# A two-layer decoder trunk on one core: softmax statistics carried between two row orders by VectorE copies instead of folding matmuls

## The reference, cut to what matters

```python
for g, (window, dilation) in enumerate(DIL_CONFIGS):
    o, l = dilated_group_attention(q[g], k[g], v[g], window, dilation, rel_table)
    outs.append(o); lses.append(l)
alpha = jax.nn.softmax(jnp.stack(lses, axis=0), axis=0)
o = jnp.sum(alpha[..., None] * jnp.stack(outs, axis=0), axis=0)
```

## Time and profile before

| | before |
|---|---|
| median of 3 runs | 1594.29 us |
| profiled execution, its own time | 1594.29 us |
| span of the profile | 1592.4 us |
| instructions | 22054 |
| TensorE matmul busy | 1576.4 us, 99% |
| VectorE busy | 919.3 us, 58% |
| ScalarE busy | 590.9 us, 37% |
| GpSimd (POOL) busy | 286.4 us, 18% |
| granted TensorE clock | 0.998 |

### The profile page before, as it was taken

One profiled execution on the slowest core, in us unless ns is written; L12 is line 12 of the kernel. 1 busy time (PEld: TensorE's weight loads), 2 busy tenths in 40 slices (PEclk: granted clock), 3 DMA queues, 4 the chain that ended last, 5 costly groups with the idle time before them and its releaser, 6 DMA issues.

```text
span 1592.4 us, 22054 instructions
## 1 busy us (share of the span) xinstructions
PE 1576.4 (99%) x8034; PEld 1296.5 (81%) x8034; DVE 919.3 (58%) x1585; ACT 590.9 (37%) x1064; POOL 286.4 (18%) x516
## 2 busy tenths in 40 slices
PE   9999999999999999999999999999999999999998
PEld 7888888888888788888888878888878888888886
DVE  5466466457456844536355766777685363545565
ACT  5324314324324522213123446676552131222344
POOL 2072473474470200000001110000020000000111
PEclk9999999999999999999999999999999999999999
DMA  6565464465443233333333332332233333333341
GB/s 166 151 166 145 141 171 129 140 166 133 120 126 112 79 104 88 100 92 97 100 92 99 99 118 69 106 92 72 73 93 98 90 104 94 92 103 92 93 116 70
DMA packets 314909, 174.84 MB, mean 110 GB/s; under 512 B 38713, under 2 KB 302450, under 8 KB 314850
## 3 DMA queue, kind: packets, MB, share of 16 engines
q1 hardware_dynamic: 300112, 158.61, 35.5%
q0 software_dynamic: 14480, 15.42, 3.5%
q10 hardware_dynamic: 258, 0.04, 0.0%
HBM read 157.11 MB, written 10.60 MB: 105 GB/s over the span
## 4 chain that ended last, share of the span: by engine, by line
PE 89%; POOL 5%; DMA 2%; DVE 1%; ACT 1%; SPq 1%; issue 0%; POOLq 0%; ACTq 0%; DVEq 0%
PE unit_out L1702 24%; PE unit_out L1704 24%; PE unit_out L1703 24%; POOL probs L902 4%; POOL sumsq L910 1%; PE attn L1850 1%; DMA w_raw<-in_a_w_qkv_dram 1%; PE attn L2098 1%; PE turned L1778 1%; PE unit_out L1869 1%; PE unit_out L1870 1%; PE unit_out L1871 1%; PE logits L1702 1%; PE misc L1778 1%; PE misc L1702 1%; PE misc L1704 1%
## 5 line engine op out<-in xcount | busy, mean ns | idle before, releaser
L1702 PE MATMUL unit_out<-act_hi,w_hi 128*128 128x512 f32 x1849 | 725.9, 393 | 1.6 <-DVE act_lo L1251 1.1
L1704 PE MATMUL unit_out<-act_hi,w_lo 128*128 128x512 f32 x1849 | 718.6, 389 | 0.0
L1703 PE MATMUL unit_out<-act_lo,w_hi 128*128 128x512 f32 x1849 | 718.0, 388 | 0.0
L928 ACT ACTIVATE w_hi<-w_raw 128x1024 fp32r<-128x1024 f32 (+3 forms) x256 | 270.9, 1058 | 464.2 <-PE unit_out L1704 368.3
L1702 PEld LDWEIGHTS unit_out<-act_hi,w_hi 128*128 128x128 f32 x1849 | 347.1, 188 | 77.3 <-DVE w_lo L1236 3.0
L1704 PEld LDWEIGHTS unit_out<-act_hi,w_lo 128*128 128x128 f32 x1849 | 347.1, 188 | 72.6
L1703 PEld LDWEIGHTS unit_out<-act_lo,w_hi 128*128 128x128 f32 x1849 | 347.4, 188 | 69.4 <-issue 0.2
L1236 DVE TENSOR_TENSOR w_lo<-w_raw,w_hi 128x1024 fp32r<-128x1024 f32 (+3 forms) x256 | 319.5, 1248 | 102.0 <-ACT w_hi L928 102.0
L902 POOL DMA_DIRECT2D probs<-blocks x448 | 220.3, 501 | 229.7 <-DVE blocks L1350 201.0
L910 POOL TENSOR_TENSOR sumsq<-sumsq,square 128x512 f32<-128x512 f32 x41 | 57.8, 1410 | 1053.6 <-ACT square L956 1051.8
L1098 ACT ACTIVATE act_hi<-hidden 128x512 fp32r<-128x512 f32 x64 | 40.5, 633 | 243.4 <-DVE hidden L1500 243.4
(11 more groups left out here) (296 smaller groups left out, 1384.2 us busy)
## 6 DMA issues: line engine op xcount, KB each, us to landing
w_raw<-in_w_ff_dram SPq DMA_DIRECT2D x128, 512.0 KB, 4.0
w_raw<-in_a_w_qkv_dram SPq DMA_DIRECT2D x56, 512.0 KB, 4.3
probs<-blocks POOLq DMA_DIRECT2D x448, 32.0 KB, 2.5
w_raw<-in_b_w_qkv_dram SPq DMA_DIRECT2D x24, 512.0 KB, 5.0
w_raw<-in_a_w_qkv_dram SPq DMA_DIRECT2D x32, 256.0 KB, 3.1
w_raw<-in_w_ple_gate_dram SPq DMA_DIRECT2D x16, 512.0 KB, 3.9
bias_tiles_b<-bias_vectors SPq DMA_DIRECT2D x16, 256.0 KB, 4.4
bias<-bias_tiles_b SPq DMA_DIRECT2D x8, 512.0 KB, 3.8
```

The lines of the kernel that those rows point to most:

```text
L928: sc.activation(weights_of(u)[0][:, 0:width, :], w_raw[par][:, 0:width, :], ACT.Copy).then_inc(hi_done, 1)
L1702: te.matmul(bank, w_k[0], hi, start=start, stop=False)
L1703: te.matmul(bank, w_k[0], lo, start=False, stop=False)
L1704: return te.matmul(bank, w_k[1], hi, start=False, stop=stop)
```

## The change

VectorE now carries the statistics by itself, in slot 2 (`merge`) and slot 4 (`near`; in the drain 4 and 6): 16 copies each, every one from 32 partitions to 32 others, of 4 elements (minimum and sum of two heads) in the first and 2 in the second. Only the last of each 16 raises a semaphore. The folds, the spreads, their waits, `fold`, `quarter` and the POOL instructions that made them are gone, and with them VectorE's waits for TensorE's folds.

```diff
-A_SPREAD, A_MERGE, A_NEAR = 1, 2, 4
+A_MERGE, A_NEAR = 2, 4
-DRAIN_SPREAD, DRAIN_MERGE, DRAIN_NEAR = 3, 4, 6
+DRAIN_MERGE, DRAIN_NEAR = 4, 6
...
+        def rows_of(a):
+
+            return slice(a * SUB, (a + 1) * SUB)
...
-            pool.memset(quarter[:, :], 0.0).then_inc(quarter_ready, 1)
-            pool.wait_ge(quarter_ready, 1)
-            for r in range(NT):
-                pool.memset(quarter[r * SUB:(r + 1) * SUB, r:r + 1], 1.0).then_inc(quarter_ready, 1)
...
-            pool.tensor_tensor(fold[:, :], ident[:, 0:SUB], ident[:, SUB:2 * SUB], ALU.add
-                               ).then_inc(fold_ready, 1)
...
-                if has_attn and i == spread_at:
+                if has_attn and i == merge_at:
 
                     wait(ve, exp_done, (s - 1).times(A_ITEMS) + 2)
-                    ve.tensor_tensor(
-                        spread_stat[:, :, :],
-                        near_stat[:, :, :].rearrange("p a b -> p (a b)").unsqueeze(2
-                            ).to_broadcast([P, 4 * NT, NT]),
-                        quarter[:, :].unsqueeze(1).to_broadcast([P, 4 * NT, NT]),
-                        ALU.mult).then_inc(spread_stat_ready, 1)
-                if has_attn and i == merge_at:
-
-                    wait(ve, far_ps, s)
-                    ve.tensor_copy(far_stat[:, :, 0, :], far_in[:, :].rearrange(
-                        "p (a b) -> p a b", a=2)).then_inc(merge_step, 1)
+                    far, near = (x.rearrange("p a (j b) -> p a j b", b=NT) for x in
+                                 (far_stat[:, :, 0, :], near_stat[:, :, :]))
+                    for b, r in itertools.product(range(NT), range(NT)):
+                        last = ve.tensor_copy(far[rows_of(b), :, :, r], near[rows_of(r), :, :, b])
+                    last.then_inc(merge_step, 1)
                     merged(s, 1)
...
                     wait(ve, share_ready, s)
-                    ve.tensor_tensor(spread_share[:, :, :],
-                                     share[:, 0, :].unsqueeze(2).to_broadcast([P, 2 * NT, NT]),
-                                     quarter[:, :].unsqueeze(1).to_broadcast([P, 2 * NT, NT]),
-                                     ALU.mult).then_inc(spread_share_ready, 1)
                 if has_attn and i == near_at:
-                    wait(ve, near_ps, s)
-                    ve.tensor_copy(near_share[:, :], near_in(has_proj)).then_inc(near_share_ready, 1)
+                    near, far = (x.rearrange("p (j b) -> p j b", b=NT) for x in (near_share[:, :], share[:, 0, :]))
+                    for b, r in itertools.product(range(NT), range(NT)):
+                        last = ve.tensor_copy(near[rows_of(r), :, b], far[rows_of(b), :, r])
+                    last.then_inc(near_share_ready, 1)
                     wait(ve, near_share_ready, s)
...
-                if has_attn and i == merge_at:
-
-                    wait(te, spread_stat_ready, s)
-                    for b in range(NT):
-                        last = te.matmul(
-                            far_in[b * SUB:(b + 1) * SUB, :].rearrange("p (a r) -> p a r", r=NT),
-                            fold[:, :],
-                            spread_stat[:, :, :].rearrange("p (a b) r -> p a b r", b=NT)[:, :, b, :],
-                            start=True, stop=True)
-                    last.then_inc(far_ps, 1)
-                if has_attn and i == near_at:
-                    wait(te, spread_share_ready, s)
-                    for r in range(NT):
-                        last = te.matmul(
-                            near_in(has_proj)[r * SUB:(r + 1) * SUB, :].rearrange("p (j b) -> p j b", b=NT),
-                            fold[:, :],
-                            spread_share[:, :, :].rearrange("p (j r) b -> p j r b", r=NT)[:, :, r, :],
-                            start=True, stop=True)
-                    last.then_inc(near_ps, 1)
```

More of the change, by code:

```diff
@@ L313, in build @@
         inv = sb("inv", [P, 4])
-        fold = sb("fold", [P, SUB])
-        quarter = sb("quarter", [P, NT])
         spare = sb("spare", [P, 1])
@@ L326, in build @@
         merge = w_raw[0][:, KC:KC + KP, :].rearrange("p k c -> p (k c)")
-        spread_stat = merge[:, 0:64].rearrange("p (a r) -> p a r", r=NT)
-        spread_share = merge[:, 64:96].rearrange("p (a b) -> p a b", b=NT)
         near_stat = merge[:, 96:112].rearrange("p (a b) -> p a b", a=2)
@@ L356, in build @@
         misc = ps("misc", [P, T])
-        far_in = logits[:, 0:4 * NT]
         def wide_bank(n):
@@ L400, in weights_of @@
             return both[:, 0, :, :], both[:, 1, :, :]
-        def near_in(has_proj):
-            return (turned if has_proj else attn)[:, 0:2 * NT]
         def scores_at(has_proj, i):
@@ L426, in merge_slots @@
         def merge_slots(has_proj):
-            return (A_SPREAD, A_MERGE, A_NEAR) if has_proj else (DRAIN_SPREAD, DRAIN_MERGE, DRAIN_NEAR)
+            return (A_MERGE, A_NEAR) if has_proj else (DRAIN_MERGE, DRAIN_NEAR)
+        def rows_of(a):
+            return slice(a * SUB, (a + 1) * SUB)
         def turned_order(x):
@@ L561, in build @@
         const_ready = sem("const_ready")
-        quarter_ready = sem("quarter_ready")
-        fold_ready = sem("fold_ready")
         gains_t = sem("gains_t")
@@ L600, in build @@
         tiles_b_ready = sem("tiles_b_ready")
-        spread_stat_ready = sem("spread_stat_ready")
-        far_ps = sem("far_ps")
         merge_step = sem("merge_step")
@@ L605, in build @@
         shift_exp = sem("shift_exp")
-        spread_share_ready = sem("spread_share_ready")
-        near_ps = sem("near_ps")
         near_share_ready = sem("near_share_ready")
@@ L860, in _ @@
                                base=0, pattern=[[-1, P]], channel_multiplier=1).then_inc(const_ready, 1)
-            pool.memset(quarter[:, :], 0.0).then_inc(quarter_ready, 1)
-            pool.wait_ge(quarter_ready, 1)
-            for r in range(NT):
-                pool.memset(quarter[r * SUB:(r + 1) * SUB, r:r + 1], 1.0).then_inc(quarter_ready, 1)
             pool.wait_ge(const_ready, 5)
-            pool.wait_ge(quarter_ready, 1 + NT)
-            pool.tensor_tensor(fold[:, :], ident[:, 0:SUB], ident[:, SUB:2 * SUB], ALU.add
-                               ).then_inc(fold_ready, 1)
[L869 to L874, removed]
             pool.memset(table_in[PIECES:PIECES + 1, :], -MASKED).then_inc(table_ready, 1)
@@ L1028, in sub_a @@
                     next_hi(u + 1)
-                _, merge_at, _ = merge_slots(has_proj)
+                merge_at, _ = merge_slots(has_proj)
                 if has_attn and i == merge_at:
@@ L1293, in start_statistics @@
             def start_statistics():
-                ve.wait_ge(quarter_ready, 1 + NT)
                 ve.wait_ge(root_ready, 1)
@@ L1332, in sub_a @@
                 start = s.reg is None and s.const == 0 and i == 0
-                spread_at, merge_at, near_at = merge_slots(has_proj)
+                merge_at, near_at = merge_slots(has_proj)
                 for ph in soft_at(has_proj, i) if has_attn else ():
@@ L1878, in sub_a @@
                 items = (s - 1).times(A_ITEMS)
-                _, merge_at, near_at = merge_slots(has_proj)
                 for ph in scores_at(has_proj, i) if has_attn else ():
@@ L1952, in sub_a @@
                     te.wait_ge(vec_ready, 4)
-                    te.wait_ge(fold_ready, NT - 1)
                 if has_proj and i == A_TURN_V[par]:
```

## The result

The changed kernel takes 1598.12 us (median of 10 runs, 1596.05 to 1600.56), the kernel before 1594.33 (10 runs, 1594.04 to 1595.57): ratio 1.0022, 95% interval 1.0014 to 1.0031. A second chip gave 1599.43 against 1594.63 (1.0028, 1.0017 to 1.0040). The forecast was 1596.7 in a range of 1591.0 to 1600.0. Two facts ask for an explanation: the profiled execution, 1596.45, lies 2.16 above its counterpart of before, almost the forecast's 2.4; and the median lies 1.7 above the profiled execution, with a spread three times that of before.

The account below looks back on a forecast made before the run. TensorE, busy 99% of the span, or what it waits for was taken as the bound, with even steps ending by POOL's chain. Odd steps -2.39, even +2.98, drain +1.78 gave +2.4 us, 1596.7, range 1591.0 to 1600.0.

Parts of the forecast that it names:

- The copy's pitch: VectorE's added copies: one at a time, 0.17 us each, so a group of 16 takes 2.7 us.
- rival 1: VectorE's copies overlap: p = 0.08, a group 1.3 us, sum -3.5, 1590.8 us; chance of faster 0.20.
- rival 2: Each VectorE copy costs p = 0.20, a group 3.2 us, sum +4.8, 1599.1 us; chance of slower 0.32.
- Even steps: Merge copies delay POOL's chain by 1.04 us: steps 2 and 4 become 1.04 longer, step 6 0.9.
- Rival 3: POOL's chain: landings spread by 1.5 us, so even steps could lose or win 1 us each by chance; no chance given.
- Odd steps: Steps 1, 5 and 7 gain 0.76 us each from two removed folds, step 3 only 0.11; sum -2.39.
- the near fold's 0.38: TensorE at the near fold: removing one fold gains 0.38 us, priced like a merge fold.
- rival 4: TensorE: the gap before a fold is not the fold's, so removal brings 0.06 us, not 0.38; chance under 0.05.
- The merge fold's 0.38: TensorE at the merge fold between two units: removing one fold gains 0.38 us.
- Near copies cost nothing: VectorE, behind the split and before the scales: later slots absorb the copies, cost nothing if p stays under 0.3.
- Drain: Last step: TensorE waits 2.22 us for scales and 0.2 for the weight split, folds give 0.64; sum +1.78.
- no difference: Outcome for the whole kernel's time, the forecast with p from 0.10 to 0.18; chance 0.48.

Follow-up runs that it names:

- e3: Changed kernel with each copy reading and writing its own 32 partitions, exchange between row orders left out: 1592.43 us, -2.30 against the kernel before.
- e11: The changed kernel unaltered, run again on another chip: 1599.43 us, +4.80 against the kernel before.
- e7: Kernel before with its folds, only the first block transposition moved to the end of slot 2: 1592.72 us, -1.75 against the kernel before.
- e8: Changed kernel with all its copies, only the first block transposition moved to the end of slot 2: 1594.98 us, +0.51 against the kernel before.
- e2: Kernel before with only the near shares carried by copies, the merge still by folds: 1597.11 us, +2.38 against the kernel before.
- e9: e6 with the near shares of steps 1 to 7 by folds again: 1589.36 us, -5.27 against the kernel before.
- e6: e5 with the first block transposition also moved to the end of slot 2: 1590.79 us, -3.68 against the kernel before.
- e5: Changed kernel with merge copies one slot earlier, before its evacuation, and the drain's near copies at slot 5's end: 1591.51 us, -2.96 against the kernel before.
- e1: Kernel before with only the merge carried by copies, the near shares still by folds: 1596.6 us, +1.87 against the kernel before.
- e10: Kernel before with 32 needless small VectorE copies added in slot 7 of each step: 1599.3 us, +4.67 against the kernel before.

## Why the prediction was right, and where it was not

**The copy's pitch** (p = 0.17, a group 2.7): measured 0.175 and 2.80. Right, and for the reason given; rival 1 (overlap) and rival 2 (p = 0.20) fell, and `e3` shows that the change of partitions decides. One detail: the first copy of a group starts on the same partitions as the instruction in front of it, so the rule of the Trainium skill holds 30 of the 32 copies of a step and not all, and the first does start 0.08 before the evacuation in front has ended (139.56 against 139.64 in step 2). It changes nothing in the sum.

**Even steps** (+1.04 by POOL's late start): the start moved by 1.07, as worked out. The step's length did not follow it everywhere, since the landing of the last block changed too: in step 2 the last issue began at 178.62 and its values at 181.99 before, 3.37 later; after, the last issue began about 0.5 before POOL's end at 179.76, and the values 1.75 later. That is -1.6, with +1.07 and 64 issues that took 0.23 less it gives the -0.78. Step 4 had like landings in both, and +0.85; step 6 became 0.39 longer and not 0.9, as POOL's issues took 0.2 and the landing 0.3 less. Rival 3 named this (1 us a step, by chance), and it took 1.6 in one. But by chance alone it is not: `e11`, the same kernel on another chip, has the landings of steps 2, 4 and 6 within 0.01 us of the first profile (1.71, 1.66 and 1.65, against 1.70, 1.66 and 1.66).

A reading that fits, and that no run tested: other transfers load weights and bias tiles near the end of a step. In step 2 before, the DMA engines move 371, 342 and 250 GB/s in the three microseconds from 177.12, and the last block is issued in their middle, at 178.62; after, this burst comes 1.2 us earlier (331, 312 and 303 GB/s from 175.92, then 88), and the last block, issued at 179.26, comes behind it. So the later start also let the block miss a collision, a term that the prediction had put at nothing. `e7` and `e8` support the chain itself.

**Odd steps** (-0.76 each for two folds in steps 1, 5 and 7, -0.11 in step 3) is the step of the prediction that failed, in three terms. First, the near fold's 0.38. Its gap looked like that of the merge fold, and I priced both by the earlier trace rows. But TensorE waited there for something else too. TensorE and VectorE in step 1 before, at the near fold, and both in step 7 after, where the fold is gone:

```profile
92.27 0.39 PE L1871 MATMUL attn<-w_hi,act_lo 128*128 128x512 f32 x1
92.58 0.25 PE L1901 MATMUL turned<-w_raw,fold 128*32 128x8 f32 x8
92.78 0.48 PE L1702 MATMUL unit_out<-act_hi,w_hi 128*128 128x512 f32 x1
...
91.90 0.73 DVE L1423 TENSOR_SCALAR heads<-unit_out,start_scale 128x512 f32<-128x512 f32 x1
```

```profile
440.82 0.39 PE L1838 MATMUL attn<-w_hi,act_lo 128*128 128x512 f32 x1
441.36 0.47 PE L1669 MATMUL unit_out<-act_hi,w_hi 128*128 128x512 f32 x1
...
440.48 0.74 DVE L1390 TENSOR_SCALAR heads<-unit_out,start_scale 128x512 f32<-128x512 f32 x1
```

Without the fold the two matmuls are still 0.54 apart, with it 0.51: the next unit writes to a bank whose values VectorE evacuates until 441.22 (92.63 before), and starts 0.14 and 0.15 after that end. This is rival 4 (the gap before a fold is not the fold's), to which the prediction gave under 0.05: true of the near fold in odd steps, false of the merge fold. `e2`'s step 7, and `e9` against `e6` in step 7 (57.32 with the near fold, 57.35 without), measure it: nothing. The merge fold's 0.38 is right (`e7` to `e9`: 57.70 to 57.32), and in even steps so is the near one's (57.32 to 56.91).

Second, the longer loop body: step 5 of `e6`, which has the pauses, is 0.7 longer than step 7, and `e9` without them has both alike. The prediction had nothing of the kind, since it counted the copies' time and not what the loop's return may cost. In step 5 of the first profile, 57.69 against 57.31 in step 7, the pauses cost 0.38 by this difference and the near fold's missing 0.38 does the rest: -0.04 instead of -0.76. In step 3, which ends by POOL's chain, they start POOL 0.8 later (23.72 of the step against 22.91): +0.36 instead of -0.11, a landing 0.7 shorter taking part of it back.

Third, step 1 (-0.10): its last block landed 4.9 us after its issue instead of 4.2, and TensorE waited 0.36 for it. So it is in the six other profiles of kernels without any fold in step 1 (`e3` to `e6`, `e8`, `e11`: 5.1 to 5.3, waits of 0.55 to 0.75), while those with a fold have 3.5 to 4.5 and no wait. What lengthens it was not tried.

**Near copies cost nothing** in the loop: nothing measured speaks against it (`e2`'s step 7 as before), but for their part in the loop's length.

**Drain** (+1.78): +2.14. The waits of TensorE for the scales came where they were forecast. From the first scores the second group of turns starts 2.10 later (513.18 - 472.66, against 510.98 - 472.56), where the sum had 1.78. `e5`, whose drain has neither wait, divides it: the folds give 0.59 (0.64 in the sum), the wait for the scales costs 2.23 (2.22), and the wait for the weight split in the merge slot costs 0.47, where I had 0.2. That last term was mis-sized.

**The median.** The two medians are 1.4 and 2.7 us above the forecast, the profiled execution is not. What was missing is that a wait of TensorE can cost more than its length. The mean granted clock of a run goes with its time:

| mean clock of the run | 0.995 | 0.996 | 0.997 | 0.998 or more |
|---|---|---|---|---|
| changed kernel, runs | 5 | 3 | 5 | 4 |
| their mean time, us | 1600.5 | 1598.9 | 1598.1 | 1596.9 |
| `e9_mixed`, runs | 0 | 0 | 0 | 6 |

In six profiles TensorE has waits of 1.7 to 2.1 us in the mixer (the changed kernel twice, `e1`, `e2`, `e8`, `e10`). Behind five of these ten waits, in four of the profiles (`e1`, `e2`, `e8` and, twice, `e11`), the clock fell to 1.2 GHz; behind the rest, in the first profile among them, it did not. In the other seven profiles no wait in the mixer is over 1.0 us and the clock of the mixer is 1.00 throughout. What decides whether the clock falls behind such a wait stays open; no run was made for it. The clock is not all of it: in `e10` the slowest run, 1600.64, has 0.998.

Of the chances, "no difference" was the likeliest at 0.48 and "slower" had 0.32. Both intervals lie above 1, and +3.8 and +4.8 us are more than the 3.2 that the prediction called the least that can be told: it came out slower. The time is near the 1599.1 of rival 2, but not by its mechanism, as the copies' pitch was not 0.20. Rival 1's own sum, 1590.8, lies just below the range that was said to take it in.

## What to carry to other kernels

Many small instructions on few partitions are paid one by one if each moves to another group of partitions: here 16 cost 2.8 us, and it is their place in an engine's order that decides whether this is seen; put them where the engine idles before an evacuation, not between one and the transposition that starts another engine's chain. Price a removed gap only after asking what else the engine would have waited for there. When a chain of transfers starts later, ask also which other transfers its end will now meet or miss. And look beyond the time of added instructions: in a hardware loop they can bring pauses at its return, and a new wait of TensorE of about 2 us can bring a stretch at half clock.

## What the runs showed of the hardware that was not expected

- With 28 more instructions in each step of VectorE's hardware loop (32 copies in place of 4 instructions; 32 more in `e10`), the engine pauses for about 2.0 and 1.6 us shortly after the loop's return, and the instruction queue moves 34 packets instead of 23. With 14 more (`e1`, `e2`, `e9`) it moves 24 and there are no pauses. In busy instructions of one turn, it sets in between 194 (`e9`, steps 5 and 6) and 222 (the changed kernel). That the pauses come from refetching a body that no longer fits is the reading that fits the packets; it was not shown.
- TensorE's clock fell from 2.4 to 1.2 GHz behind five of ten waits of 1.8 to 2.1 us; one such stretch cost 1.6 us in the drain of `e11`.
- The last of 64 block moves led to its values 1.75 us after its issue in step 2 of the changed kernel and 3.37 in step 2 of the kernel before, with the same code for the moves; two profiles of the changed kernel agree on the 1.75.
